# A two-layer decoder trunk in fp32: inputs laid out feature-major, 32-column sample products, and a new order of the first head and of the gate

## The chip, the cores and the metric

The kernel runs on one core of a Trainium2 chip. The metric is the device time of one execution in microseconds. TensorE, VectorE, ScalarE and GpSimd run their own instruction streams and meet at semaphores; SyncE (SP) issues the DMAs. In the profile PE is a TensorE matmul instruction, PEld its weight load, DVE is VectorE, ACT is ScalarE, SPq the queue on SyncE.

## The reference

The trunk has two layers and 1024 features. It takes 528 prompt positions (16 learned meta tokens and 512 tokens) and 8 single sample tokens, each with states of its own. Everything is fp32.

```python
def retention_chunk(q, k, v, s_prev, log_gamma):      # layer 0, 4 heads, dk 256, dv 512
    scores = einsum('bhnd,bhmd->bhnm', q, k) * decay_mask
    inner = einsum('bhnm,bhme->bhne', scores, v)
    cross = einsum('bhnd,bhde->bhne', q, s_prev) * cross_decay
    s_new = exp(log_gamma * L) * s_prev + einsum('bhmd,bhme->bhde', k * k_decay, v)
    return inner + cross, s_new

def retention_mixer(h, ...):
    q, k, v, g = split(h @ w_in)                      # q, k rotated in pairs of features
    o = normalise(retention(q, k, v))                 # mean and variance over dv
    return (silu(g) * o) @ w_out

def shortconv_mixer(h, ...):                          # layer 1
    bg, cg, xin = split(h @ w_in, 3)
    return (bg * dwconv(concat(conv_state, cg * xin))) @ w_out

def conv_ffn(h, ...):                                 # in both layers, d_ff 2816
    up, gate = split(h @ w_in, 2)
    return (silu(dwconv(concat(ffn_state, up)) + b) * gate) @ w_down

for i in range(2):
    x = x + mixer_i(rms_norm(x)); x = x + conv_ffn(rms_norm(x))
return rms_norm(x), new_ret_states, new_conv_rows, new_ffn_rows
```

For a sample the state matters: `cross` is q (1 x 256) times its own 256 x 512 state in each head, and the new state is the decayed old one plus the outer product of k and v. There are 8 x 4 such states of 512 KB each, read and written once.

## The kernel before

The residual `x_res` (X) lies feature-major: 8 tiles of 128 features by 536 columns (528 prompt, 8 sample). A projection is computed as weights (stationary, 128 x 128) times activations (moving, two halves of 260 to 268 columns, `spans`). To keep fp32 accuracy each operand is split into a rounded high part and the rest (`h_hi`, `h_lo`, `w_hi`, `w_lo`), and `three` issues three products of fp32r for each pair of tiles, all accumulating in PSUM: high by high, low by high, high by low. That makes six instructions for one weight tile and one output slot (two banks).

Weights come in units of 128 x 1024 (512 KB). SP loads a unit into one of two slots of `w_raw`, ScalarE rounds it into `w_hi` (L850, `split_hi`), VectorE subtracts into `w_lo` (L1091, `split_lo`), and TensorE uses it from one of four slots. The unit is freed by `unit_done`, and `hi_ready`/`lo_ready` count up to the next load (L273, L277). The order of units, and of every instruction of each engine, is written out by hand; each engine has one program with waits on counts.

The first head. The weights lie in their own row-major arrays, so a unit is gathered by strided DMAs, and the q and k weights are read with a step of two to part the rotary pairs. x arrives as rows in two halves of five DMAs, and small tables (norm gains, conv weights, states) as rows as well. TensorE transposes the tiles of x (L474, 40 instructions) into PSUM, VectorE copies them into X (L1114), ScalarE writes `h_hi` (L855) and the square (L860), VectorE `h_lo` (L1097) and the running sum of squares (L1101, L1104). The queries (`first_q`) are computed between those transposes; `rows_tiles` transposes the tables (L485, L490). `first_k` computes the keys and, between them, the mean of squares (`statistic`, L454) and its row-wise copy (L527). The root, its reciprocal (L1163) and the scaling of the cos and sin tables by it (L1169, L1170) stand ahead of the rotation of Q and K (`rotate`, L1178 to L1181), so q and k are scaled by the norm inside the rotation.

A head. Then come: V (L565, 120 products of 512 columns), the transposes of K (L572), the scores (L587, L595), the KV product for the prompt's state (L602, plain fp32), the inner products of scores and V in four groups `dt` (L633, L635), and the gate: four parts per weight unit and half, units 8 and 9 in one slot pair, 10 and 11 in the other. Q, K, V, scores, states and statistics use plain fp32 or fp32r as the code says. The output projection (units 12 to 15) works on `ret_z_hi` and `ret_z_lo`.

The samples. The eight states of a head pass through a ring of four slots, `state_ring` (S). For each state ScalarE rounds it (`state_hi`, L896) and VectorE takes the rest (`state_lo`, L1210) into `state_split_a` or `_b`; `sample(b)` multiplies it by `dec_q_spread` (QM), in which each sample's q stands in one of 128 columns, as high part in columns 0 to 63 and as low part in 64 to 127. This is

```python
def sample(b):
    pe.wait_ge(s_lo, 8 * h + (b + 1))
    for e in range(2):
        for part in range(2):
            out = mm(PS[:, 1, :], QM[:, e, b * NB:b * NB + P], (SA, SB)[b % 2][:, part, e * DV:(e + 1) * DV], ...)
```

with four fp32r instructions of 512 columns for each sample (L611): two samples ahead of the inner products, one behind each `dt`, two among the gate's first parts. VectorE then updates the state in place (L1249) with the outer product that ScalarE made from v broadcast over the partitions (`outer`, L925); SP stores it (L335) and loads state b + 4 into its slot (L343). ScalarE copies the sums out (`OS`, L942), and a product with `row_sum` (SEL, L658) adds the two rows of each sample and transposes them.

The gate's statistics. TensorE computes the mean over the channels (`statistic(3, MEAN_V, TMP[:, 4, ...])`, L454) after the first pair of parts of unit 9. VectorE subtracts it (L1258), ScalarE squares (L946), VectorE sums (L1263). The second statistic stands between unit 10 and unit 11. Then VectorE: split of unit 12, the gate's scaling (L1267), split of unit 13, the reciprocal of the root (L1288), normalising and the product with silu (L1271, L1277), `z_rest` into `ret_z_lo` (L1281), for which the output projection waits.

The end. After the last FFN TensorE transposes y and the last rows of the FFN's up projection (`state_rows`, L708), and SP stores four blocks of y, y_sample and three DMAs of FFN rows (`ffn_states`).

## Time and profile before

| | before |
|---|---|
| median of 3 runs | 1552.12 us (1551.85 to 1553.26) |
| the profiled execution | 1551.32 us, its span 1549.5 us |
| granted clock of TensorE, mean | 0.998 |
| instructions on TensorE | 11511 matmuls, 11511 weight loads |
| busy share TensorE, VectorE, ScalarE | 99%, 52%, 35% |
| moved by DMA | 171.92 MB, mean 111 GB/s |

The span runs from the first to the last instruction; some microseconds of an execution lie around it. Matmuls overlap, so the time of one is read from the distance of starts, not from its duration. A busy share near 100% says that the engine always had an instruction in hand.

### The profile page before, as it was taken

The numbers are of one execution on the slowest core, as the hardware profiler recorded it, in microseconds if no ns is written. First come the engines' busy times: TensorE is split into PE (matmuls) and PEld (weight loads), VectorE is DVE, ScalarE is ACT, GpSimd is POOL, SyncE is SP. The second block draws the span as 40 slices with busy tenths as digits, with TensorE's granted clock in tenths as the row PEclk, the third lists the DMA queues.
The fourth block names the chain that finished last, engine by engine and source line by source line (L and its number), as shares of the span: only waits on it lengthen the run. The fifth ranks groups of instructions, "written<-read, shape, count | busy, mean of one in ns | idle before, by whom it ended". The sixth has DMA issues, their size and how long they took to land.

```text
span 1549.5 us, 27952 instructions
## 1 busy us (share of the span) xinstructions
PE 1528.8 (99%) x11511; PEld 1458.6 (94%) x11511; DVE 808.7 (52%) x1046; ACT 547.6 (35%) x743; POOL 1.8 (0%) x17
## 2 busy tenths in 40 slices
PE   8999999999999999999999999999999999999997
PEld 7879969987997899999999999999999999999997
DVE  6667437545744696555555233544455555554222
ACT  4264136215412654333333123322333333333222
POOL 0000000000000000000000000000000000000000
PEclk9999999999999999999999999999999999999999
DMA  7362434335252532232232222322322322322321
GB/s 223 101 232 79 161 137 177 124 103 208 81 182 82 218 96 92 85 95 85 91 95 83 94 96 82 96 92 86 96 93 85 95 82 94 95 87 94 96 88 59
DMA packets 119544, 171.92 MB, mean 111 GB/s; under 512 B 5358, under 2 KB 91894, under 8 KB 118382
## 3 DMA queue, kind: packets, MB, share of 16 engines
q1 hardware_dynamic: 119462, 170.71, 33.8%
q8 instruction: 66, 1.08, 0.3%
q14 instruction: 16, 0.13, 0.0%
HBM read 149.35 MB, written 21.55 MB: 110 GB/s over the span
## 4 chain that ended last, share of the span: by engine, by line
PE 97%; DVE 1%; issue 0%; ACT 0%; DMA 0%; SPq 0%; DVEq 0%; ACTq 0%
PE ps L420 79%; PE ps L565 7%; PE ps L633 3%; PE ps L602 2%; PE ps L611 2%; PE ps L595 1%; PE ps L454 1%; PE ps L587 1%; PE ps L474 1%; DMA x_rows<-in_x_sample_dram 0%; PE ps L817 0%; DVE rms L1163 0%; DVE w_lo L1091 0%; PE ps L635 0%; PE ps L658 0%
## 5 line engine op out<-in xcount | busy, mean ns | idle before, releaser
L850 ACT ACTIVATE w_hi<-w_raw 128x1024 fp32r<-128x1024 f32 x228 | 241.1, 1059 | 755.7 <-PE ps L420 663.9
L1091 DVE TENSOR_TENSOR w_lo<-w_raw,w_hi 128x1024 fp32r<-128x1024 f32 x228 | 278.2, 1222 | 387.0 <-ACT w_hi L850 386.9
L420 PE MATMUL ps<-h_hi,w_hi 128*128 128x264 f32 (+2 forms) x2304 | 472.6, 286 | 3.5 <-DVE w_lo L1091 2.8
L420 PE MATMUL ps<-h_lo,w_hi 128*128 128x264 f32 (+2 forms) x2304 | 468.5, 285 | 0.0
L420 PE MATMUL ps<-h_hi,w_lo 128*128 128x264 f32 (+2 forms) x2304 | 468.0, 284 | 0.0
L420 PEld LDWEIGHTS ps<-h_hi,w_hi 128*128 128x128 f32 x2304 | 359.5, 190 | 5.8 <-DVE w_lo L1091 3.0
L420 PEld LDWEIGHTS ps<-h_hi,w_lo 128*128 128x128 f32 x2304 | 358.5, 190 | 0.2 <-issue 0.2
L420 PEld LDWEIGHTS ps<-h_lo,w_hi 128*128 128x128 f32 x2304 | 358.3, 190 | 0.0
L420 PE MATMUL ps<-z_hi,w_lo 128*128 128x264 f32 (+1 forms) x832 | 167.9, 283 | 0.0
L420 PE MATMUL ps<-z_lo,w_hi 128*128 128x264 f32 (+1 forms) x832 | 167.8, 283 | 0.0
L420 PE MATMUL ps<-z_hi,w_hi 128*128 128x264 f32 (+1 forms) x832 | 167.5, 283 | 0.0
L420 PEld LDWEIGHTS ps<-z_hi,w_hi 128*128 128x128 f32 x832 | 128.4, 188 | 0.0
L420 PEld LDWEIGHTS ps<-z_hi,w_lo 128*128 128x128 f32 x832 | 128.2, 188 | 0.0
L420 PEld LDWEIGHTS ps<-z_lo,w_hi 128*128 128x128 f32 x832 | 128.1, 188 | 0.0
L1361 DVE TENSOR_TENSOR tmp<-ps,rms 128x528 f32<-128x528 f32 (+1 forms) x44 | 29.0, 700 | 77.4 <-PE ps L420 77.4
L1342 DVE TENSOR_TENSOR tmp<-ps,rms 128x528 f32<-128x528 f32 (+1 forms) x44 | 29.0, 701 | 69.5 <-PE ps L420 69.5
L565 PE MATMUL ps<-w_hi,h_hi 128*128 128x512 f32 x160 | 63.2, 395 | 0.9 <-DVE tmp L1178 0.9
L565 PE MATMUL ps<-w_hi,h_lo 128*128 128x512 f32 x160 | 63.2, 395 | 0.0
L565 PE MATMUL ps<-w_lo,h_hi 128*128 128x512 f32 x160 | 63.1, 394 | 0.0
L1249 DVE SCALAR_TENSOR_TENSOR state_ring<-state_ring,decay,gate 128x1024 f32<-128x1024 f32 x32 | 40.8, 1283 | 22.7 <-ACT gate L925 20.0
L420 PE MATMUL ps<-ret_z_hi,w_lo 128*128 128x264 f32 x256 | 52.0, 285 | 0.0
L420 PE MATMUL ps<-ret_z_hi,w_hi 128*128 128x264 f32 x256 | 52.0, 284 | 0.0
(177 smaller groups left out, 1379.5 us busy)
## 6 DMA issues: line engine op xcount, KB each, us to landing
w_raw<-in_w_ffn_in_dram SPq DMA_DIRECT2D x88, 512.0 KB, 3.5
w_raw<-in_w_ret_in_dram SPq DMA_DIRECT2D x48, 512.0 KB, 3.7
w_raw<-in_w_ffn_out_dram SPq DMA_DIRECT2D x44, 512.0 KB, 3.7
state_ring<-in_state_ret_dram SPq DMA_DIRECT2D x32, 512.0 KB, 5.5
out_ret_s_dram<-state_ring SPq DMA_DIRECT2D x32, 512.0 KB, 2.9
w_raw<-in_w_sc_in_dram SPq DMA_DIRECT2D x24, 512.0 KB, 3.5
w_raw<-in_w_ret_out_dram SPq DMA_DIRECT2D x16, 512.0 KB, 3.4
v_bcast<-v_scratch SPq DMA_DIRECT2D x8, 1024.0 KB, 5.6
```

The source lines that it names most:

```text
L420: out = mm(PS[:, 2 * s + half, at:at + n_col], a, b[:, lo:lo + n_col], start=first and n == 0, stop=last and n == 2)
L454: out = mm(PS[:, 2 * s + half, at:at + n_col], ones[:], src[:, lo:lo + n_col], start=True, stop=True)
L474: out = pe.transpose(PS[:, 2 * X_SLOT[k] + b // 4, (b % 4) * P:(b % 4) * P + n], XN[0:n, b, k * P:(k + 1) * P], IDENT[0:n, 0:n])
L565: out = mm(PS[:, banks[b], :], a, c, start=k == 0 and q == 0, stop=k == KD - 1 and q == 2)
L602: out = mm(PS[:, 6 + e, :], KN[0:mn, j, e * P:(e + 1) * P], V[0:mn, j, :], start=j == 0, stop=j == 4)
L611: out = mm(PS[:, 1, :], QM[:, e, b * NB:b * NB + P], (SA, SB)[b % 2][:, part, e * DV:(e + 1) * DV], start=b == 0 and e == 0 and part == 0, ...
L633: mm(PS[:, 2 * s + half, a - n0:n1 - n0], V[0:mn, j, vt], PR[0:mn, PCOL[j] + a - m0:PCOL[j] + n1 - m0], start=j == 0, stop=j == js[-1])
L850: fn(WH[:, c % NS, :], RAW[:, c % NR, :], ACT.Copy).then_inc(hi_ready, 1)
L1091: tt(WL[:, c % NS, :], RAW[:, c % NR, :], WH[:, c % NS, :].bitcast(F32), ALU.subtract).then_inc(lo_ready, 1)
L1249: stt(S[:, b % 4, :], S[:, b % 4, :], DEC[:, TP + 5:TP + 6], G[:, at:at + 1024], ALU.mult, ALU.add).then_inc(s_upd, 1)
L1342: tt(halves(TMP[:, t, 0:n_in]), slot(PAIR_A[t], w), halves(R[:, c0:]), ALU.mult).then_inc(up_read, 1)
L1361: tt(halves(TMP[:, t, 0:n_in]), slot(PAIR_B[t], w), halves(R[:, c0:]), ALU.mult).then_inc(gate_read, 1)
```

## The change

Inputs are laid out ahead of the launch: `x_all` (feature-major x), `model_consts` and `ffn_consts` (feature-major tables), and `w_units`, in which each weight unit is one contiguous 128 x 1024 block in the order of its use, with the q and k features parted, so the step of two is gone. x is loaded tile by tile straight into X; unit 0 comes in two halves. The FFN's and the conv's last rows leave in the layout they have on chip and are reordered outside. In the first head the order of units is q and k of the first half, then of the second; keys follow queries with a lag of two tiles; q and k are rotated with unscaled tables and scaled afterwards; the statistic comes after all keys. The samples are computed in two calls of four, unsplit, in plain fp32 with 32 weight columns, each to its own group of 32 partitions. In the gate, three parts of the second slot go first, the second call of samples follows the sixth part, the `SEL` products and the first statistic come later in unit 9. `spans` (264 + 260 columns for 524) is as before.

```diff
+TILE = 32
-X_SETUP = KD
+X_SETUP = 0
+K_LAG = 2
...
-            QM = sb("dec_q_spread", [P, 2, 192], F32R, scope=s2)
+            QM = sb("dec_q_spread", [P, 2, 96], scope=s2)
...
@@ sync: start
-            x_half(0)
-            in_heads(0, 0)
-            x_half(1)
+            sp.dma_start(RAW[:, 0, 0:512], w_all[0, :, 0:512]).then_inc(half_in, 16)
+            x_tile(0)
+            sp.dma_start(CD[:], io["model_consts"]).then_inc(const_in, 16)
+            sp.dma_start(RAW[:, 0, 512:], w_all[0, :, 512:]).then_inc(raw_in[0], 16)
+            x_tile(1)
             in_heads(0, 1)
...
+            x_tile(2)
+            x_tile(3)
+            in_heads(0, 2)
+            x_tile(4)
+            in_heads(0, 3)
+            for k in range(5, KD):
+                x_tile(k)
...
@@ sync: states of a head
-                for b in range(NB):
+                def store(b):
                     sp.wait_ge(s_upd, 8 * h + (b + 1))
...
-                    if b == 4:
-                        sp.wait_ge(kv_ready, h + 1)
...
+                for b in range(4):
+                    store(b)
+                    if b > 0:
+                        reload(b - 1)
+                reload(3)
+                sp.wait_ge(kv_ready, h + 1)
...
+                for b in range(4, NB):
+                    store(b)
...
@@ tensor: first head
+                for k in range(KD):
...
+                    pe.wait_ge(h_lo, k + 1)
+                    for e in range(2):
+                        out = part(2 * (k // 4), PAIR_A[e], k, e)
...
+                    if k >= K_LAG:
+                        n = k - K_LAG
...
+                        part(2 * (n // 4) + 1, PAIR_B[0], n, 0)
...
+                pe.wait_ge(ss_sum, 7)
+                pe.wait_ge(rope, 4)
+                statistic(1, MEAN_D, TMP[:, 2, :], T // 2).then_inc(stat_done, 1)
...
-                    for b in range(5):
+                    for b in ((2, 3, 4, 0, 1) if first else range(5)):
...
+                        if first and n == 4 and b == 0:
+                            pe.wait_ge(rstd, 1)
...
@@ tensor: samples and gate
-                def sample(b):
+                def samples(b0):
...
-                    pe.wait_ge(s_lo, 8 * h + (b + 1))
+                    for c in range(4):
+                        pe.wait_ge(s_in[c], 32 * h + 4 * b0 + 16)
                     for e in range(2):
...
+                        for c in range(4):
+                            at = (b0 + c) * NB
+                            out = mm(PS[TILE * c:TILE * c + TILE, 1, :], QM[:, e, at:at + TILE], S[:, c, e * DV:(e + 1) * DV],
+                                     start=b0 == 0 and e == 0, stop=b0 == 4 and e == 1)
+                    out.then_inc(samp_done, 4)
...
+                samples(0)
...
-                pe.wait_ge(o_ready, 4 * h + 4)
...
+                for n, (kk, e) in enumerate(((0, 1), (1, 1), (2, 1), (0, 0), (1, 0), (2, 0), (3, 0), (3, 1))):
+                    if n == 0:
+                        pe.wait_ge(o_ready, 4 * h + 2)
+                    if n == 3:
+                        pe.wait_ge(o_ready, 4 * h + 4)
+                    out = gate_part(8, PAIR_A, kk, e)
+                    if n == 5:
+                        samples(4)
...
+                    if kk == 0:
+                        pe.wait_ge(sel_ready, 2)
+                        pe.wait_ge(os_ready, h + 1)
...
+                    if kk == 2:
+                        pe.wait_ge(o_sum, 6 * h + 6)
+                        statistic(3, MEAN_V, TMP[:, 4, 0:N_RET], N_RET // 2).then_inc(gstat_done, 1)
...
@@ vector: first head, and updates of the states
+            def first_scale():
...
+                for t in (Q, K):
+                    for e in range(2):
+                        tt(t[:, e, :], t[:, e, :], R[:], ALU.mult).then_inc(qk_scaled, 1)
...
-                    dve.wait_ge(s_lo, 8 * h + (b + 1))
+                    dve.wait_ge(samp_done, 8 * h + 4 * (b // 4 + 1))
...
+                for b in range(4):
+                    update(b)
+                dve.wait_ge(o_ready, 4 * h + 4)
+                channel_sum(slice(C_RET, TP), 0)
+                update(4)
+                update(5)
                 dve.wait_ge(ot_done, h + 1)
...
+                update(6)
+                update(7)
```

On ScalarE `state_hi` goes, `outer(4)` and `outer(5)` follow the first two output copies, and `outer(6)` and `outer(7)` the copy of `OS`. The stores of the FFN's and conv's last rows move from the end into the stream of weight loads, one DMA each.

## Rows read from the trace of the kernel before

**Rows 1.** The page: busy time of TensorE, and the chain by engine.
```profile
PE 1528.8 (99%) x11511; PEld 1458.6 (94%) x11511; DVE 808.7 (52%) x1046; ACT 547.6 (35%) x743; POOL 1.8 (0%) x17
...
PE 97%; DVE 1%; issue 0%; ACT 0%; DMA 0%; SPq 0%; DVEq 0%; ACTq 0%
```

**Rows 2.** Timeline of TensorE, first head: start, duration, line, names, count.
```profile
13.13 0.78 PE L420 MATMUL ps<-h_hi,w_hi 128*128 128x268 f32 x2 [0.69 <-issue]
13.71 0.65 PE L420 MATMUL ps<-h_lo,w_hi 128*128 128x268 f32 x2
...
15.50 0.65 PE L420 MATMUL ps<-h_hi,w_lo 128*128 128x268 f32 x2
...
35.81 1.07 PE L454 MATMUL ps<-tmp,mean_d 128*128 128x268 f32 x4
...
37.73 0.53 PE L420 MATMUL ps<-h_hi,w_hi 128*128 128x268 f32 x2
```

**Rows 3.** The same timeline, V products of the first head and what follows.
```profile
53.69 0.50 PE L565 MATMUL ps<-w_hi,h_hi 128*128 128x512 f32 x1 [0.31 <-DVE tmp L1178]
...
76.10 1.25 PE L572 MATMUL ps<-ident,k_rot 128*128 128x128 f32 x10
```

**Rows 4.** Windows: engines' busy time (instructions), PEclk, DMA share, GB/s.
```profile
0.00:4.00 4.00, 0.98 (x8) 0.93 (x8) 0.34 (x2) 1.49 (x2) 1.83 (x17) 1.00 0.35 80
4.00:8.00 4.00, 0.73 (x4) 0.71 (x4) 0.00 (x0) 0.00 (x0) 0.00 (x0) 1.00 0.98 344
```

**Rows 5.** Timeline of ScalarE and VectorE in the first head.
```profile
9.47 0.74 ACT L855 ACTIVATE h_hi<-x_res,model_consts 128x536 fp32r<-128x536 f32 x1 [7.23 <-DVE x_res L1114]
...
11.80 1.23 DVE L1091 TENSOR_TENSOR w_lo<-w_raw,w_hi 128x1024 fp32r<-128x1024 f32 x1 [0.48 <-ACT w_hi L850]
...
13.57 0.77 DVE L1097 SCALAR_TENSOR_TENSOR h_lo<-x_res,model_consts,h_hi 128x536 fp32r<-128x536 f32 x1
```

**Rows 6.** Timeline of TensorE, second head: first and last of 96 pairs.
```profile
161.70 0.41 PE L420 MATMUL ps<-h_hi,w_hi 128*128 128x268 f32 x2
...
185.36 0.41 PE L420 MATMUL ps<-h_hi,w_lo 128*128 128x268 f32 x2
```

**Rows 7.** Timeline of TensorE, first head: KV product, two samples, what follows.
```profile
82.60 9.43 PE L602 MATMUL ps<-v_rows,k_rows 128*128 128x512 f32 x20
91.96 1.20 PE L611 MATMUL ps<-state_split_a,dec_q_spread 128*128 128x512 f32 x4
...
93.93 2.96 PE L633 MATMUL ps<-scores,v_rows 128*128 128x268 f32 x16
```

**Rows 8.** Timeline of TensorE, second head: both statistics and the output projection.
```profile
257.84 1.06 PE L454 MATMUL ps<-tmp,mean_v 128*128 128x264 f32 x4
...
266.00 1.05 PE L454 MATMUL ps<-tmp,mean_v 128*128 128x264 f32 x4
266.69 0.60 PE L420 MATMUL ps<-h_hi,w_hi 128*128 128x264 f32 x2
...
275.66 0.40 PE L420 MATMUL ps<-ret_z_hi,w_hi 128*128 128x264 f32 x2
```

**Rows 9.** Timeline of VectorE in the same stretch.
```profile
262.20 1.52 DVE L1263 TENSOR_TENSOR tmp<-tmp 128x528 f32<-128x528 f32 x2
...
267.82 3.45 DVE L1288 RECIPROCAL tmp<-tmp 128x528 f32<-128x528 f32 x1 [0.60 <-ACT tmp L863]
...
274.18 0.70 DVE L1281 TENSOR_TENSOR ret_z_lo<-ret_out,ret_z_hi 128x528 fp32r<-128x528 f32 x1
```

**Rows 10.** The page's DMA issues: engine, count, KB each, us to landing.
```profile
state_ring<-in_state_ret_dram SPq DMA_DIRECT2D x32, 512.0 KB, 5.5
out_ret_s_dram<-state_ring SPq DMA_DIRECT2D x32, 512.0 KB, 2.9
```

**Rows 11.** Timeline of the queue on SyncE at the end.
```profile
1543.88 0.72 SPq L402 DMA_DIRECT2D out_y_sample_dram<-y_rows  x1
...
1546.38 0.82 SPq L383 DMA_DIRECT2D out_ffn_s_dram<-ffn_state_rows  x1
```

More of the change, by code:

```diff
@@ L443, in pair_of_k @@
                         for e in range(2):
-                            out = three(slots[e], w, lhs_pair(c + half, kk, e, step),
+                            out = three(slots[e], w, lhs_pair(c + half, kk, e),
                                         h_cols(HH, k, c0, 2 * w), h_cols(HL, k, c0, 2 * w), k == 0, k == KD - 1)
@@ new lines, in head @@
+                for kk in range(4):
+                    for e in range(2):
+                        out = gate_part(9, PAIR_A, kk, e)
+                    if kk == 0:
+                        pe.wait_ge(sel_ready, 2)
+                        pe.wait_ge(os_ready, h + 1)
+                        pe.sem_inc(rows_seen, 1)
+                        for dt in range(4):
+                            row = mm(PS[:, 0, dt * NB:(dt + 1) * NB], OS[:, dt * P:(dt + 1) * P], SEL[:],
+                                     start=True, stop=True)
+                        row.then_inc(ot_done, 1)
+                    if kk == 2:
+                        pe.wait_ge(o_sum, 6 * h + 6)
+                        statistic(3, MEAN_V, TMP[:, 4, 0:N_RET], N_RET // 2).then_inc(gstat_done, 1)
@@ L1506, in shape_constants, with weight_units, put @@
     return {"cos": np.cos(ang).astype(np.float32), "sin": np.sin(ang).astype(np.float32), "decay": decay}
[L1509 to L1511 removed]
+def weight_units(w_ret_in, w_ret_out, w_sc_in, w_sc_out, w_ffn_in, w_ffn_out):
+    units = np.empty((U_ALL, P, UNIT), np.float32)
+    def put(u, block):
+        rows, cols = block.shape
+        units[u] = block.reshape(rows // P, P, cols).transpose(1, 0, 2).reshape(P, UNIT)
+    pairs_apart = np.concatenate([np.arange(0, DK, 2), np.arange(1, DK, 2)])
+    for h in range(HEADS):
+        u = U_HEAD * h
+        for n in range(4):
+            half, part = (n // 2, n % 2) if h == 0 else (n % 2, n // 2)
+            put(u + n, w_ret_in[0, 512 * half:512 * half + 512][:, part * D + h * DK + pairs_apart])
+        for n in range(4):
+            put(u + 4 + n, w_ret_in[0, 256 * n:256 * n + 256, 2 * D + h * DV:2 * D + (h + 1) * DV])
+            at = 2 * D + VDIM + h * DV + 256 * (n // 2)
+            put(u + 8 + n, w_ret_in[0, 512 * (n % 2):512 * (n % 2) + 512, at:at + 256])
+            put(u + 12 + n, w_ret_out[0, h * DV:(h + 1) * DV, 256 * n:256 * n + 256])
+    for l in range(2):
+        for i in range(JF // 2):
+            for n in range(4):
+                at = 256 * i + (n // 2) * DFF
+                put(U_FFN_IN[l] + 4 * i + n, w_ffn_in[l, 512 * (n % 2):512 * (n % 2) + 512, at:at + 256])
+        for n in range(22):
+            g, v = divmod(n, 11)
+            put(U_FFN_OUT[l] + n, w_ffn_out[l, 256 * v:256 * v + 256, 512 * g:512 * g + 512])
+    for i in range(4):
+        for n in range(6):
+            at = 256 * i + (D, 2 * D, 0)[n // 2]
+            put(U_SC_IN + 6 * i + n, w_sc_in[0, 512 * (n % 2):512 * (n % 2) + 512, at:at + 256])
+    for n in range(8):
+        put(U_SC_OUT + n, w_sc_out[0, 512 * (n % 2):512 * (n % 2) + 512, 256 * (n // 2):256 * (n // 2) + 256])
+    return units
```

513 lines of the change are left out of this document (197 added, 316 removed).

## The prediction

> **What bounds the kernel now.** I read the page's busy shares and its chain first. TensorE is busy for 1528.8 us of 1549.5, and the chain that ended last lies on it for 97% [rows 1]. So an edit on VectorE, ScalarE or a queue is worth something only where TensorE waits for it, and a TensorE instruction taken away or added counts in full. The weights' layout in memory, the splits of the states and the fewer VectorE operations are therefore worth nothing by themselves. What is left is four places: the start, where TensorE does its first projection product only at 13.1 us [rows 2]; the sample products inside each of the four heads [rows 7]; the order of the gate with its two statistics [rows 8]; and the tail after the last product [rows 11]. I went through each on the timeline of TensorE, then of the engine that feeds it there.
>
> **Part 1, the start.** Before, x arrives as rows and is transposed 40 times on TensorE; the first product starts at 13.1 us, and the V products end at 76.1 [rows 2, 3]. After, x arrives feature-major, and what the first product needs is half of unit 0 (0.26 MB), tile 0 of x (0.27 MB) and the constants (0.10 MB). The windows show 80 GB/s in the first 4 us, which is 0.32 MB, and 344 GB/s in the next 4 [rows 4]: 0.63 MB is there at 4 + 0.31/0.344 = 4.9 us. Then ScalarE rounds tile 0 (0.74 us) and VectorE takes the rest (0.77 us) [rows 5]: TensorE starts at about 6.5 us, 6.6 us earlier.
>
> From there the work is 8 tiles of x, 4 output slots and 6 instructions each, 192 instructions. Pairs of them follow each other at 0.249 us in a later head (23.66 us for the 95 pairs between its first and its last row), so 0.1245 each, 23.9 us [rows 6]. The first ones go slower: from 13.71 to 15.50 there are four pairs, 0.448 us a pair, 0.224 each [rows 2]. That is what the lower of the two clock levels (1.2 GHz against 2.4) would give, though the window's granted clock reads 1.00 at such a coarse view. Before, this lasted from 13.1 to about 16.8 us; I take the same 3.7 us, in which half the work is lost at 0.1 us for each of 17 instructions, 1.7 us. The queries and keys end at 6.5 + 23.9 + 1.7 = 32.1 us. The statistic and the five row statistics cost 37.73 - 35.81 = 1.9 us, as before [rows 2]: 34.0. V is 120 products; 96 of them ran from 53.69 to 76.10, 0.2334 each [rows 3], 28.0 us: V ends at 62.0 us against 76.1. That is **-14.1 us**.
>
> Can the feeders keep up? For each tile ScalarE rounds and squares, about 0.74 us each, VectorE takes the rest and adds a square, about 0.77 each, and for four units each of them splits, up to 1.23: at most 8 x 1.54 + 4.9 = 17.2 us on VectorE and less on ScalarE [rows 5]. TensorE needs 2.2 us a tile and 25.6 us in all, so it is the slowest after the first tile. All of x and units 0 to 3, 4.3 MB, is in by 4 + 4.0/0.344 = 15.6 us, where tile 7 is wanted at about 22 us [rows 4]. The loads of units 2 and 3 stand in the queue ahead of tiles 4 to 7 and wait for the splits of units 0 and 1, at 6 to 9 us; late by 2 us, they would still be hidden. Before the V products, the late scaling by the root costs VectorE a reciprocal (3.5 us) and six products of 0.7, after the rotation of K at 36 us; that ends at 44 us, and the first that wants it is the transposes of K at 62. So it is hidden; were it not, it would cost 7.7 us once. The bounds: -16 if the first bytes arrive as early as the constants are ready (2.4 us earlier than I took), -11 if each unit's load delays a tile.
>
> **Part 2, the sample products.** Before, one sample is four 512-column instructions; two samples cost 93.93 - 91.96 = 1.97 us [rows 7], so eight cost 7.9 us per head. After, the state isn't split, and the product is plain fp32, with 32 weight columns going to partition groups 0, 32, 64, 96: 16 products per head. Plain fp32 goes in two instructions each: the KV product shows 20 instructions for 10 products, 9.36 us, 0.468 each [rows 7]. So there are 32 instructions of 0.468. No row of before shows products in four column groups, so I bound it.
> - All serial: 32 x 0.468 = 15.0 us per head.
> - All four groups side by side: two calls, two halves e, two passes, 8 x 0.468 = 3.7 us.
> - Pairwise: if instructions start in order and the second pass of a product has to wait for the first one in its own group, the next group's first pass runs beside the second pass of the one before. Eight products take 9 pass times, 4.2 us, both calls 8.4 us.
>
> To each I add 0.2 us for every call, by which the first pair behind a block of plain fp32 is longer (0.60 us at 266.69, where a pair in a row lasts 0.41) [rows 6, 8]. I take the pairwise one, since the passes of a product are adjacent in the stream of [rows 7]: 8.8 against 7.9 us, +0.9 us per head, **+3.7 us**. The ends are -3.8 and +7.5 us per head, -15 and +30 us in all.
>
> The Trainium skill ("TensorE: Matmul & The Clock Gate", the part on packing small matmuls) says that products in different 32-column strips run concurrently, each starting some 4 ns after the one before, and that they start and end strictly in order. No row here shows it; for one instruction per strip it would give the side-by-side case, and for two the pairwise case. Another page ("TensorEngine Tiling (Array Packing)", Key Properties) says that changing the tiling mode drains the engine, which speaks against the edit; it has no price there, and I stay with the 0.2 us.
>
> **Part 3, the order in the gate.** Before, the first statistic comes after the first pair of unit 9's parts, at 257.84, the second one at 266.00, and the output projection at 275.66 [rows 8]. After, the first statistic stands two pairs of parts later (2 x 1.46 = 2.9 us), while all behind it stays. So TensorE has 2.9 us less of other work between the statistic and what comes from it: 5.25 us to the second statistic, and 17.82 - 2.9 = 14.9 us to the projection. VectorE's chain between them: it ends the sum of squares at 263.72, 5.9 us after 257.84, and has the first z_lo ready at 274.88, 17.0 us after. It idled 0.60 us before the reciprocal, for a root that comes earlier now [rows 9], so 16.4 us. TensorE's cover ends before that: 5.9 - 5.25 = 0.65 us at the second statistic and 0.85 more at z_lo, 1.5 us per head, **+6.0 us**. The bounds are 0 (if the four squares or the split behind them go ahead of where they stood) and 2.4 us per head (if the 0.60 isn't given back and z_lo of the third tile is late as well). I take the worked-out value.
>
> The rest of the gate rewrite costs nothing by the rows: three parts now go ahead of the wait for the last output copy. The second call of the samples needs states 4 to 7 back in the ring 16.8 us after the first call ends (four inner groups of 3.1 us and six parts of 0.73). The four updates take 5.2 us, a store 2.9, its successors 3, and a load 5.5 to land [rows 10]: 13.4 to 15.4 us. That is hidden with 1.4 us to spare.
>
> **Part 4, the tail and the middle.** Before, SP issues y_sample at 1543.88 and then three more stores, the last at 1546.38, which leaves 3.1 us to the end at 1549.5 [rows 11]. VectorE's last y rows don't move. After, y_sample is the last store: **-2.5 us**, bounds -1.5 and -3. The transposes of the FFN's last rows go too, a few tenths of a microsecond: costed at nothing.
>
> **Sum.** -14.1 + 3.7 + 6.0 - 2.5 = -6.9 us. The profiled execution took 1551.3 us (span 1549.5), which gives 1544.4; the median of the runs lies 0.8 us above it, so **1545 us**.
>
> **The rivals.**
> - *Four strips side by side.* The samples cost 4.1 us per head, 1545 - 3.7 - 15 = 1526 us. For it: it is what tiles are for. Against: each product is two instructions on the same strip.
> - *Strips don't overlap.* 32 x 0.468 + 0.4 = 15.4 us per head, +30 us where I took +3.7: 1571 us, slower. The samples eat up the other gains from (14.1 - 6.0 + 2.5) / 4 = 2.65 us above the 7.9 of before on, that is from 10.5 us per head. For it: only such rows as [rows 7] exist, all serial. Against: a 32-column product uses a quarter of the array.
> - *The reorder costs nothing*, because VectorE's queue has slack that I took for full: 1539 us.
> - *The second call of the samples waits for the ring.* If the loads land 4 us later than in [rows 10], TensorE stands still 2.6 us per head, and more where the second half of the broadcast is late: 1555 to 1557 us. It decides from 1.4 us of lateness. For it: the loads come in a row behind the stores, and a landing of 5.5 us is a median. Against: one store and the KV copy now come after the last reload.
> - *The start is not gained*, since the queue of loads feeds the eight tiles too slowly: at worst -6.6 us is all that is left, 1552 us, no change.
>
> **How the numbers follow.** Pairwise strips with the gate's wait 0.42; the same without the wait 0.13; side by side 0.16; serial 0.17; the ring late 0.07; the start not gained 0.05. The range from 1526 to 1557 us holds all but the serial case and some edges. Within 0.2% is about 3 us, which is what a measurement of this kernel can tell from no change. Faster: nearly all of the first, the second and the third, 0.71; the same 0.07; slower 0.22.
>
> **What the profile after should show.** The first L420-like product at 6 to 7 us, the last of V at about 62. Per head 32 sample instructions of 32 columns over 8 to 9 us, overlapping in pairs. Idle of TensorE of 0.6 us before the second mean statistic and 0.9 before the products of ret_z. The last store issued near 1537. I am wrong first if the sample products take 4 or 15 us per head, next if the start isn't near 6.5 us.

## The result, and the profile after

| | before | after |
|---|---|---|
| median | 1552.09 us (1551.85 to 1553.26) | 1532.38 us (1531.99 to 1532.77, 4 runs) |
| ratio | | 0.9872, 95% interval 0.9854 to 0.9889 |
| span of the profiled execution | 1549.5 us | 1530.4 us |
| granted clock of TensorE, mean | 0.998 | 0.997 |

The change takes 19.7 us off. The forecast was 1545 us, a gain of 7 us: 12.6 us above the measured time, which lies in the lower part of the stated range (1526 to 1557 us). First the page of the kernel after: busy time, the chain by engine, and the two DMA rows of the ring.

```profile
PE 1504.1 (98%) x11428; PEld 1428.8 (93%) x11428; DVE 765.0 (50%) x1004; ACT 515.7 (34%) x710; POOL 1.7 (0%) x17
...
PE 89%; DMA 4%; DVE 4%; ACT 1%; issue 1%; SPq 0%; DVEq 0%; ACTq 0%
...
state_ring<-in_state_ret_dram SPq DMA_DIRECT2D x32, 512.0 KB, 5.6
out_ret_s_dram<-state_ring SPq DMA_DIRECT2D x32, 512.0 KB, 2.7
```

TensorE was 97% of the chain [rows 1] and is 89% now: DMA and VectorE have come onto it, with 4% each. That says before any timeline that the change didn't only shorten TensorE's work but also opened waits. The idle times of TensorE name them: who waits on which line, for what, us in total, times, the longest.

```profile
PE ps L376 <- DVE h_lo L1024: 7.6, 3, 6.6
PE ps L537 <- DMA state_ring<-in_state_ret_dram: 3.8, 4, 1.6
PE ps L409 <- DVE tmp L1182: 2.4, 4, 0.6
PE ps L376 <- DVE x_res L1231: 2.1, 1, 2.1
PE ps L376 <- DVE ret_z_lo L1200: 2.0, 4, 0.6
```

In the kernel after, L376 is the line of the projections' products (without V), L537 that of the sample products, L409 that of the statistics. The first row is the start. The third and the fifth are the two waits in the gate that were forecast. The second, the samples' second call waiting for the ring in every head, was a rival only. The fourth happens once, at the end of the second head, and before had a like one (its stretch there took 26.33 us against 23.36 in the others, and takes 25.87 against 23.59 now).

Right behind it TensorE's granted clock falls to 0.50, the lower of its two levels (1.2 GHz of 2.4), for 3.4 us (in the line of this window it is the third number from the end):

```profile
287.00:290.40 3.40, 3.40 (x16) 3.40 (x16) 0.19 (x1) 0.00 (x0) 0.00 (x0) 0.50 0.55 182
```

The stretch from there to V takes 25.32 us where it takes 23.69 in the other heads, 1.6 us more. The kernel before has the same dip (25.65 against 23.90), so it plays hardly any part in the 19.1 us; but some of the executions below lack it, and are shorter by as much.

Now the timeline of TensorE, start to the end of the first head, to be laid beside [rows 2, 3, 7, 8].

```profile
6.58 0.79 PE L376 MATMUL ps<-h_hi,w_hi 128*128 128x268 f32 x2 [6.58 <-DVE h_lo L1024]
...
9.76 0.81 PE L376 MATMUL ps<-h_hi,w_hi 128*128 128x268 f32 x2 [0.15 <-DVE h_lo L1024]
...
12.65 0.48 PE L376 MATMUL ps<-h_hi,w_hi 128*128 128x268 f32 x2 [0.82 <-DVE h_lo L1024]
...
33.75 1.06 PE L409 MATMUL ps<-tmp,mean_d 128*128 128x268 f32 x4
...
35.67 0.50 PE L487 MATMUL ps<-w_hi,h_hi 128*128 128x512 f32 x1
...
64.00 1.25 PE L496 MATMUL ps<-ident,k_rot 128*128 128x128 f32 x10
...
79.87 1.93 PE L537 MATMUL ps<-state_ring,dec_q_spread 128*32 128x512 f32 x16
81.72 3.06 PE L558 MATMUL ps<-scores,v_rows 128*128 128x268 f32 x16
...
98.77 0.40 PE L376 MATMUL ps<-h_hi,w_lo 128*128 128x264 f32 x2
99.74 1.92 PE L537 MATMUL ps<-state_ring,dec_q_spread 128*32 128x512 f32 x16 [0.57 <-DMA state_ring<-in_state_ret_dram]
101.60 0.51 PE L376 MATMUL ps<-h_hi,w_hi 128*128 128x264 f32 x2
...
114.44 1.13 PE L409 MATMUL ps<-tmp,mean_v 128*128 128x264 f32 x4 [0.60 <-DVE tmp L1182]
...
124.91 0.48 PE L376 MATMUL ps<-ret_z_hi,w_hi 128*128 128x264 f32 x2 [0.60 <-DVE ret_z_lo L1200]
```

What the reader is to see: the V products end at 64.0 us where they ended at 76.1; a call of sixteen sample instructions takes 81.72 - 79.87 = 1.85 us; and three gaps open behind it, which each cost some 0.2 us more than their bracket (the idle time) says, since pairs follow each other at 0.245 us (98.77 to 99.74 is 0.97, so 0.73 are lost). Of such a figure at a sample call some 0.08 us are there without any wait: so much is left wherever the states are in time.

Where the 19.1 us of span went, from the starts of the same steps in both timelines:

| stretch | before | after | difference |
|---|---|---|---|
| to the end of V, first head | 76.10 | 64.00 | -12.1 |
| transposes of K to the gate, 4 heads | 34.38, 34.32, 34.31, 34.38 | 30.55, 30.48, 30.49, 30.55 | -15.3 |
| gate to the output projection, 4 heads | 27.86 x3, 27.87 | 30.36, 30.38, 30.59, 31.36 | +11.2 |
| the rest of the heads | | | -0.5 |
| layer 1 and the FFNs, to the transposes of y | 955.83 | 955.50 | -0.3 |
| from there to the end | 15.2 | 13.1 | -2.1 |
| sum | | | -19.1 |

### The profile page after: what moved, and what is told of

Same layout as the page of the kernel before. It is cut to its first block, busy times and chain, and to the rows that moved or that the text cites. A ratio compares the mean times of both kernels' runs of the same rounds, so it can differ in the third digit from the quotient of the medians.

```text
span 1530.4 us, 27659 instructions
## 1 busy us (share of the span) xinstructions
PE 1504.1 (98%) x11428; PEld 1428.8 (93%) x11428; DVE 765.0 (50%) x1004; ACT 515.7 (34%) x710; POOL 1.7 (0%) x17
## 4 chain that ended last, share of the span: by engine, by line
PE 89%; DMA 4%; DVE 4%; ACT 1%; issue 1%; SPq 0%; DVEq 0%; ACTq 0%
PE ps L376 76%; PE ps L487 7%; PE ps L526 2%; DMA out_ret_s_dram<-state_ring 2%; DMA state_ring<-in_state_ret_dram 1%; PE ps L537 1%; DVE tmp L1207 1%; PE ps L519 1%; DVE w_lo L999 1%; PE ps L511 1%; ACT tmp L860 1%; PE ps L409 0%; DMA w_raw<-in_w_units_dram 0%; DVE ret_out L1190 0%; DVE ret_out L1177 0%
## 5 line engine op out<-in xcount | busy, mean ns | idle before, releaser
L376 PE MATMUL ps<-h_hi,w_hi 128*128 128x264 f32 (+2 forms) x2304 | 473.0, 287 | 9.7 <-DVE h_lo L1024 7.6
L376 PE MATMUL ps<-h_lo,w_hi 128*128 128x264 f32 (+2 forms) x2304 | 468.6, 285 | 0.0
L376 PE MATMUL ps<-h_hi,w_lo 128*128 128x264 f32 (+2 forms) x2304 | 467.3, 284 | 0.0
L376 PEld LDWEIGHTS ps<-h_hi,w_hi 128*128 128x128 f32 x2304 | 357.7, 189 | 14.6 <-issue 12.2
L376 PEld LDWEIGHTS ps<-h_lo,w_hi 128*128 128x128 f32 x2304 | 357.7, 189 | 0.0
L376 PEld LDWEIGHTS ps<-h_hi,w_lo 128*128 128x128 f32 x2304 | 357.6, 189 | 0.0
L376 PE MATMUL ps<-z_hi,w_lo 128*128 128x264 f32 (+1 forms) x832 | 167.9, 283 | 0.0
L376 PE MATMUL ps<-z_lo,w_hi 128*128 128x264 f32 (+1 forms) x832 | 167.8, 283 | 0.0
L376 PE MATMUL ps<-z_hi,w_hi 128*128 128x264 f32 (+1 forms) x832 | 167.5, 283 | 0.0
L376 PEld LDWEIGHTS ps<-z_hi,w_hi 128*128 128x128 f32 x832 | 128.4, 188 | 0.0
L376 PEld LDWEIGHTS ps<-z_hi,w_lo 128*128 128x128 f32 x832 | 128.2, 188 | 0.0
L376 PEld LDWEIGHTS ps<-z_lo,w_hi 128*128 128x128 f32 x832 | 128.0, 188 | 0.0
L840 ACT ACTIVATE gate<-v_bcast,dec_k 128x512 f32<-128x512 f32 x64 | 41.4, 713 | 45.5 <-DMA v_bcast<-v_scratch 33.5
L376 PE MATMUL ps<-ret_z_hi,w_hi 128*128 128x264 f32 x256 | 52.6, 287 | 2.0 <-DVE ret_z_lo L1200 2.0
```

Of the source, the lines that this page charges most:

```text
L376: out = mm(PS[:, 2 * s + half, at:at + n_col], a, b[:, lo:lo + n_col], start=first and n == 0, stop=last and n == 2)
L840: fn(G[:, at:at + DV], VB[:, b, :], ACT.Copy, scale=KD8[:, e, b:b + 1]).then_inc(samp_kv, 1)
```

## The experiments

**How far do the strips run side by side?** A strip is one of the four groups of 32 partitions to which a product of 32 weight columns writes. Three kernels differ from the one after in the order or the place of the sample products. In the first, all products of a call go to the partitions 0 to 31; in the second, to two strips. Both sum samples together that belong apart, so their sample outputs are not the reference's; the sample products and their operands are the same, and the copy and the `SEL` products behind them take only the partitions that were written.

```diff
# one_strip
-out = mm(PS[TILE * c:TILE * c + TILE, 1, :], QM[:, e, at:at + TILE], ...
-         start=b0 == 0 and e == 0, stop=b0 == 4 and e == 1)
+out = mm(PS[0:TILE, 1, :], QM[:, e, at:at + TILE], ...
+         start=b0 == 0 and e == 0 and c == 0, stop=b0 == 4 and e == 1 and c == 3)
# two_strips
+out = mm(PS[TILE * (c % 2):TILE * (c % 2) + TILE, 1, :], QM[:, e, at:at + TILE], ...
+         start=b0 == 0 and e == 0 and c < 2, stop=b0 == 4 and e == 1 and c > 1)
# strip_by_strip
-                    for e in range(2):
-                        for c in range(4):
+                    for c in range(4):
+                        for e in range(2):
```

> The changed kernel, but all four products of a sample call go to the same 32 partitions (the sums of the four samples are mixed, so this output is not the reference's; the rest is as it was). Theory A, column strips work side by side: a call of 16 instructions took 1.9 us because four strips ran at once; on one strip they follow each other at 0.468 us, 7.5 us a call, 5.6 us more, twice in four heads: +45 us, about 1577 us. Theory B, a plain-fp32 instruction with 32 weight columns is short by itself (0.12 us), wherever it goes: no change, 1532 us.

> The same, but the four products alternate between two groups of 32 partitions (sums of two samples each are mixed, so this output is not the reference's). Theory A: 16 instructions over two strips, 8 pass times of 0.468 = 3.7 us a call, 1.9 us more than with four: +15 us, about 1547 us. Theory B: 1532 us.

> The changed kernel with the two loops of a sample call exchanged: four instructions in a row for strip 0, then four for strip 1, and so on. Same products, same strips. Theory C (that of my prediction, starts in order, and a pass waits for the one before it on its strip): only the last pass of a strip overlaps the first of the next, 13 pass times, 6.1 us a call, 4.2 us more: +34 us, about 1566 us. Theory D, the strips take their work independently of the order in the stream: no change, 1532 us.

One run each: 1572.98 us, 1545.74 us and 1530.64 us. The timeline of TensorE at the first call, for one strip,

```profile
80.13 7.05 PE L537 MATMUL ps<-state_ring,dec_q_spread 128*32 128x512 f32 x16
87.11 3.06 PE L558 MATMUL ps<-scores,v_rows 128*128 128x268 f32 x16
```

for two strips (its call lasts to 83.25),

```profile
79.69 3.63 PE L537 MATMUL ps<-state_ring,dec_q_spread 128*32 128x512 f32 x16
```

and for four, ordered strip by strip:

```profile
80.17 1.94 PE L537 MATMUL ps<-state_ring,dec_q_spread 128*32 128x512 f32 x16
82.05 3.06 PE L558 MATMUL ps<-scores,v_rows 128*128 128x268 f32 x16
```

So a call takes 6.98, 3.56 and 1.88 us, and 1.85 in the kernel after: about halved with each doubling of the strips. On one strip an instruction costs 6.98 / 16 = 0.44 us (the expectation had taken 0.468), on four 0.12. The 1530.64 us of the third kernel are no gain by its order: its profiled span is 1.7 us shorter than that of the kernel after, and in it the clock didn't fall behind the second head (23.80 us from there to V instead of 25.32). The last kernel decides between the forecast's mechanism and its rival. With two halves of two passes each on one strip, adjacent in the stream, instructions that start in order would leave little to overlap; yet the call is as short as before. The trace, asked for the sample instructions that touch 80.22 to 80.60 us (in flight; count, duration ns, first and last start), shows four already at work together in this kernel too:

```profile
L537 PE MATMUL ps<-state_ring,dec_q_spread x4: 617/617/617, 80.2 to 80.2; 128*32 128x512 f32 x4
```

The next four start at 80.6, then at 81.1 and 81.5. On one strip alone the trace has one start every 0.43 us, so four that start together are on four strips. The records don't name the strip, but they do show that the order of the stream had changed: within a four the starts lie 13 to 14 ns apart here and 7 ns in the kernel after, twice as far with twice as many instructions of one strip in a row. The pairwise case, on which the forecast rests, falls: a second pass does wait for the first one on its own strip, but it doesn't hold up what stands behind it for another strip. That each strip works off its own instructions is my reading of this; that the order of the two loops makes no difference to the time of a call is measured. The Trainium skill ("TensorE: Matmul & The Clock Gate", the part on packing small matmuls) says that products in different strips run concurrently; the runs agree, and with two passes a product as well. The Trainium skill says in the same part that products start strictly in order, each some 4 ns after the one before. Four starts together, out of a stream with four instructions in a row for each strip, do not bear out the order, and the distances are 7 and 13 to 14 ns.

**The samples and the gate without the rest.** The kernel before, with the sample calls, ring order, state updates and gate of the one after; inputs, first head and tail stay.

```diff
 # samples_and_gate_only, against the kernel before
-C_LO = 64
+TILE = 32
-QM = sb("dec_q_spread", [P, 2, 192], F32R, scope=s2)
+QM = sb("dec_q_spread", [P, 2, 96], scope=s2)
# and in short: sample(b) on SA, SB, state_hi and state_lo go;
# samples(0), samples(4) on S come; store, reload, update, outer and the gate's order as after
```

> The kernel before with only the new samples (unsplit, 32 columns, two calls, ring order, updates) and the new gate order; inputs, weight loads, first head's start and the end are those of before. If the changed kernel's trace is read rightly, the heads gave 4.6 us and the start and end the other 14 to 15: the profiled span falls from 1549.5 by 4 to 6 us, the ratio is 0.996 to 0.997. Rival: the gains of samples show only with contiguous loads, because the strided loads crowd the ring's reloads: then the ring wait before the second call grows and the time is that of before or above it.

1547.96 us in the median of 8 runs (1545.86 to 1549.61) against 1552.07, ratio 0.9974 (0.9963 to 0.9985), a little above the 0.996 to 0.997 expected; the profiled span fell by 5.0 us, as expected. It is a gain by itself, where the forecast booked 9.7 us of loss for these two parts. In its trace the first V products end 2.6 us later than before, with the transposes of x starting only at 9.16 us behind a load of x's rows; the transposes of K to the gate take 30.54, 30.49, 30.49 and 30.55 us, as after, and the gate 30.04, 29.60, 31.33 and 29.72. These two stretches gain 6.1 us here and 4.1 in the kernel after, whose ring waited longer (4.4 us against 2.3). So the gain of the heads is this part's, and the start's 12 us, which are not there, belong to the other part.

**The kernel after once more**, beside three kernels that each move one thing in the gate, timed on the same chip.

```diff
 # second_call_later
-                    if n == 5:
+                    if n == 7:
                         samples(4)
 # stat_earlier
-                    if kk == 2:
+                    if kk == 1:
                         statistic(3, MEAN_V, TMP[:, 4, 0:N_RET], N_RET // 2)
 # unit13_later (VectorE)
-                split_lo(NS + 9, U_HEAD, h)
                 dve.wait_ge(g_std, h + 1)
...
                 z_rest(1)
+                split_lo(NS + 9, U_HEAD, h)
                 normalise(2)
```

> The changed kernel once more, beside the three that follow, so that they are compared on one chip: 1532 us, ratio 0.987.

> The changed kernel with the second sample call behind all eight parts of unit 8 and not behind six: 1.46 us more cover for the ring. In the changed kernel TensorE waits 0.7, 0.7, 1.1 and 1.9 us there. Theory A, what follows hangs on VectorE's chain that starts with this call (updates, mean, z_lo), so that a later call moves all of it: the ring wait goes, the waits at the second statistic and at z_lo grow by as much, and only the head with 1.9 us gains: 0 to 1 us less, 1531 to 1532 us. Theory B, each wait counts by itself: 4 us less, 1528 us.

> The changed kernel with the first statistic of the gate one pair of parts (1.46 us) earlier. VectorE now idles 0.69 us for it after the last update. Theory A (chain): that idle time is what can be gained, so the two waits of TensorE (0.76 and 0.77 us per head) fall to some 0.8 in sum: 2.8 us less, 1529.5 us. Theory B, the waits are the missing cover of 1.46 us in full: both vanish, 6 us less, 1526 us. Theory C, no gain, since the root or the squares on ScalarE set the end.

> The changed kernel, in which VectorE splits unit 13 behind the second z_lo and not ahead of the reciprocal: the split is 1.14 us of VectorE's chain before the first z_lo, and unit 13 is wanted 2.9 us after the projection starts. Theory A (chain): the wait at the projection (0.77 us per head) goes, that at the second statistic stays: 3 us less, 1529 us. Theory B: the wait only moves to the products of unit 13 or to the third z_lo: no change, 1532 us.

| kernel | median (runs), us | ratio to before | gate to projection, 4 heads |
|---|---|---|---|
| changed_again | 1531.32 (1530.51 to 1531.84) | 0.9871 (0.9855 to 0.9888) | 30.80, 29.58, 29.83, 30.07 |
| second_call_later | 1528.79 (1528.35 to 1528.97) | 0.9853 (0.9837 to 0.9870) | 29.80, 29.65, 29.64, 30.00 |
| stat_earlier | 1528.67 (1527.88 to 1530.45) | 0.9857 (0.9841 to 0.9874) | 29.81, 28.83, 29.36, 29.54 |
| unit13_later | 1531.59 (1531.19 to 1532.04) | 0.9871 (0.9855 to 0.9888) | 29.68, 29.89, 29.48, 29.96 |

The ring's wait differs from execution to execution: by the distances of the starts TensorE lost 0.73, 0.87, 1.07 and 1.73 us there in the first profile of the kernel after, and 1.18, 0.09, 0.28 and 0.43 in that of `changed_again`. So gains of one or two microseconds are read from the waits as well as from the medians.

*The second call two parts later* gives 2.5 us, between the 0 to 1 us of the one theory and the 4 us of the other. The waits of TensorE in it:

```profile
PE ps L409 <- DVE tmp L1182: 2.4, 4, 0.6
PE ps L376 <- DVE ret_z_lo L1200: 2.0, 4, 0.6
```

Both are as they were, and the ring's wait is down to 0.2 us, from 1.3 in the same view of `changed_again`; by the distances of the starts it is 0.6 after 2.0. Of the 1.6 us between the two profiled spans 1.3 are thus the ring's. That the rest of the 2.5 us between the medians is the ring's too is likely, since its wait varies so much, and not shown. A wait for the ring is not paid back at the statistic: what arrives late there stays lost.

*The statistic one pair of parts earlier* gives 2.7 us, as its theory A had it: the wait at the second statistic (2.4 us) is gone, the one at `ret_z_lo` is not. The term of the forecast for the first of the two waits is shown.

*The split of unit 13 out of the way* removes the wait at `ret_z_lo` (2.6 us by the distances) and gains nothing. Its waits:

```profile
PE ps L376 <- DVE gate L1186: 2.8, 4, 0.7
PE ps L537 <- DMA state_ring<-in_state_ret_dram: 2.7, 4, 0.9
```

TensorE now stands still inside the projection, for the fourth part of the gate, which VectorE scales 1.2 us later behind the moved split; from the projection to the next head it takes 24.3 us instead of 23.6, 2.5 us over the four heads. VectorE is full there (in the first head of the kernel after it has no gap above 0.1 us from 111.5 to 129 us), and a wait taken away at one product comes back at the next.

**The first call of the samples ahead of the KV product**, so that the ring has 9.4 us more. On ScalarE the KV copy goes behind the four outer products, or it would wait for a product that is now later.

```diff
 # first_call_earlier (TensorE)
                 pe.wait_ge(kn_ready, 5 * h + 5)
+                pe.wait_ge(qm_ready, 3 * h + 3)
+                samples(0)
...
                 out.then_inc(kv_done, 1)
-                pe.wait_ge(qm_ready, 3 * h + 3)
-                samples(0)
 # (ScalarE)
-                act.wait_ge(kv_done, h + 1)
-                fn(KV[:], PS[:, 6:8, :], ACT.Copy).then_inc(kv_ready, 1)
                 outer(2)
                 outer(3)
+                act.wait_ge(kv_done, h + 1)
+                fn(KV[:], PS[:, 6:8, :], ACT.Copy).then_inc(kv_ready, 1)
```

> The changed kernel with the first sample call ahead of the KV product, and ScalarE's copy of the KV sums behind the fourth outer product, so that the updates can start as soon as v is broadcast and not 3.2 us later: the ring's stores and reloads go 3 us earlier. Theory A, the second call waits for the chain of updates, stores and reloads: its waits of 0.7 to 1.9 us go, 4.4 us less (1527.5 us). Theory B, the reloads wait for the DMA engines, which are full in that stretch whatever the order: at most 1 us less.

> The changed kernel with the three: first call ahead of the KV product, first statistic one pair earlier, unit 13 split later. If each gives what its theory A says and none stands in another's way: 4.4 + 2.8 + 3.1 = 10.3 us less, about 1522 us, ratio to before 0.980 to 0.981. If they share a chain, less than the sum: 1525 us.

1526.34 us (1525.95 to 1527.51, 5 runs), ratio 0.9842 (0.9828 to 0.9855), with no wait for the ring left in its trace: 5.0 us below changed_again, 4.5 by the ratios. Not all of that is the ring's. Of the 4.3 us between the two profiled spans (1528.5 and 1524.2), the gates hold 1.6 (30.07 to 29.68 in the mean), the stretches from the transposes of K to the gate 0.5, the start 0.5, and 1.5 lie in the stretch from the second head's end to the next V (25.31 against 23.80), where the edit touches nothing. Those 1.5 us are the clock: in this execution it stayed up, though TensorE had stood still for 2.35 us just before, longer than the 2.11 us ahead of the dip in the kernel after.

```profile
287.00:290.40 3.40, 3.40 (x29) 3.40 (x29) 0.00 (x0) 0.00 (x0) 0.00 (x0) 1.00 0.84 280
```

In `first_and_stat`, below, the clock falls to 0.50 again from 284.8 to 288.2 us, and the stretch takes 25.30. The five executions of `first_call_earlier` fall into two groups accordingly: spans of 1524.1 and 1524.2 us at a mean granted clock of 0.999, and of 1525.4 and 1525.5 at 0.998. What the early call is worth lies between the 1.6 us of the gates and the 4.4 that the ring took in the first profile of the kernel after.

`all_three` (this, `stat_earlier` and `unit13_later` together) ran in 1523.47 us (1523.39 to 1525.65), ratio 0.9823 (0.9810 to 0.9836): some 8 us gained of the 10.3 that the sum of the parts gave. In its trace the gate takes 28.2 us in each head, and the wait for `gate` is there again with 2.7 us in 4.

**Without the moved split.** The last two kernels leave the split of unit 13 where it was: `first_and_stat` is `first_call_earlier` with `kk == 1`, and `first_stat_second` has `n == 7` besides.

> The kernel after, with the first call of the samples ahead of the KV product (the KV copy behind the four outer products on ScalarE) and the first mean statistic one pair of parts earlier; the split of unit 13 stays ahead of the gate's scaling, other than in all_three. Theory A, the two waits that go are independent and the split of unit 13 moved away buys nothing: first_call_earlier (1526.3) minus the 2.4 to 2.7 us of the wait at the second statistic, so 1524 us, with the wait for ret_z_lo (2.0 us in 4) still there, no wait for the gate, projection to next head 23.6 us; 1523 to 1524.5 and equal to all_three. Theory B, the split of unit 13 in its old place lengthens VectorE's chain again once the statistic is early: the wait for ret_z_lo grows to 4 us in 4, and 1526 us.

> first_and_stat, and the second call of the samples behind the last of unit 8's parts instead of behind the sixth. The wait for the ring is gone already with the first call in its new place. Theory A, the move of the second call was worth its 2.5 us in second_call_later by the ring's wait alone: now no change, within 0.5 us of first_and_stat. Theory B, it has a gain of its own (fewer changes between products): another 1.5 to 2.5 us, 1521.5 to 1522.5 us.

1524.92 us (1523.87 to 1525.21), ratio 0.9827 (0.9813 to 0.9841), and 1524.36 us (1524.11 to 1525.22), ratio 0.9825 (0.9811 to 0.9839). The traces are as the first theories had them: the wait for `ret_z_lo` stays, that for the ring and that at the statistic are gone. The times are a little beside their bounds (1523 to 1524.5 us, and within 0.5 us of each other). What the early call and the early statistic give adds up, and the second call's place is worth nothing that these runs can tell once the ring is in time. The waits of `first_and_stat`:

```profile
PE ps L376 <- DVE h_lo L1023: 7.2, 1, 7.2
PE ps L376 <- DVE w_lo L998: 2.5, 1, 2.5
PE ps L376 <- DVE ret_z_lo L1199: 2.0, 4, 0.6
```

The intervals of these two and of `all_three` overlap, so none of them is the best; all three stand about 0.5% below the kernel after (0.9825 / 0.9872). In the profiled executions, which all three have the dip of the clock, `all_three` spans 1523.7 us and the other two 1522.5 and 1522.4: the moved split shows no gain there either.

## Why the prediction was right or wrong

| step | forecast | measured |
|---|---|---|
| Part 1, the start | -14.1 | -12.1 |
| Part 2, the sample products | +3.7 | -16.7 |
| Part 3, waits at the statistic and at z_lo | +6.0 | +5.7 |
| Part 3, the ring | 0 | +4.4 |
| gate and inner groups beside these | 0 | +2.5 |
| the heads' rest and the middle | 0 | -0.8 |
| Part 4, the tail | -2.5 | -2.1 |
| sum (of the unrounded terms) | -6.9 | -19.1 |

**Part 2 failed, and it alone decides the size.** "I take the pairwise one, since the passes of a product are adjacent in the stream" was the choice. The two calls of a head take 1.85 and 1.86 us, 3.7 in all where 8.8 were forecast and 7.9 stood before: -4.2 us per head, -16.7. That is the rival of four strips side by side, whose term of -15 the forecast had worked out and given 0.16. The rule behind the choice has two halves, and no row supported either. That a second pass waits for the first one on its strip holds: `one_strip` has one start every 0.43 us. That everything behind it in the stream waits with it fails: in the kernel after and in `strip_by_strip` four start together. The price at a change of shape, taken as 0.2 us a call, is 0.1: the first pair behind a call takes 101.95 - 101.60 = 0.35 us where others take 0.245.

**Part 1 was right in its mechanism and 2.0 us too large.** The first product came at 6.58 us, forecast 6.5, and the statistic and row statistics took 35.67 - 33.75 = 1.92 us, forecast 1.9. The queries and keys ended at 33.75, not 32.1. TensorE waited for `h_lo` twice, and by the distances of the pairs lost 0.37 us at 9.76 and 0.98 at 12.65. The text had weighed the engines' sum of work against TensorE's; it should have gone through their order. ScalarE, in its own timeline, had stood still for the loads of the second half of unit 0 and of unit 1, each with a tile behind it (the rounding of tile 1 at 8.08 us, of tile 2 at 10.90),

```profile
7.31 0.63 ACT L794 ACTIVATE w_hi<-w_raw 128x512 fp32r<-128x512 f32 x1 [1.80 <-DMA w_raw<-in_w_units_dram]
8.08 0.74 ACT L790 ACTIVATE h_hi<-x_res,model_consts 128x536 fp32r<-128x536 f32 x1
9.39 1.06 ACT L763 ACTIVATE w_hi<-w_raw 128x1024 fp32r<-128x1024 f32 x1 [0.57 <-DMA w_raw<-in_w_units_dram]
10.36 0.64 ACT L786 ACTIVATE x_squares<-x_res 128x536 f32<-128x536 f32 x1
10.90 0.73 ACT L790 ACTIVATE h_hi<-x_res,model_consts 128x536 fp32r<-128x536 f32 x1
```

and VectorE has the split of unit 1 ahead of its tile 2:

```profile
10.49 1.23 DVE L999 TENSOR_TENSOR w_lo<-w_raw,w_hi 128x1024 fp32r<-128x1024 f32 x1 [0.78 <-ACT w_hi L763]
11.73 0.78 DVE L1024 SCALAR_TENSOR_TENSOR h_lo<-x_res,model_consts,h_hi 128x536 fp32r<-128x536 f32 x1
```

The tile that TensorE wants at 11.7 us is ready at 12.5. The forecast's bound of -11 had named this, a load of a unit that delays a tile, and its sum had left it out. Another 0.3 us are the V products, 28.3 us against 28.0; the last 0.2 are spread over the rest. This reading of the queue was not tried in a run. The 1.7 us for the slow start held: until 10.4 us the pairs are some 0.45 us apart (7.17, 7.61, 8.06), then 0.25. The windows read a granted clock of 1.00 there, but where they read 0.50, behind the second head, the pairs are just as far apart (287.29, 287.74, 288.18), so the lower level, as the forecast took it, is the likely reading.

**Part 3 was right for the two waits.** By the distances of the starts each head loses 0.76 us at the second statistic, and 0.77, 0.57, 0.59 and 0.71 at z_lo, where 0.65 and 0.85 were forecast: 5.7 us over four heads. The sum is closer than its terms, of which one was too small and one too large. `stat_earlier` took the first of them away and got its 2.7 us. It is the kind of step that the timelines carry well: all instructions were in the trace of before, and only their order changed.

**The ring was costed at nothing and cost 4.4 us** in this execution (2.0 in the other). The rival was there (0.07) with the point from which it decides, 1.4 us of lateness. That slack was wrong in the sum itself: the four terms written down, 5.2 us for the updates, 2.9 for a store, 3 for its successors and 5.5 for a load, add up to 16.6 us and not to 13.4 to 15.4, so only 0.2 of the 16.8 us were left. The rows were the second flaw: a median over 32 transfers [rows 10] stood for the ones that end the chain. The chain of work in head 1 of the kernel after, in order of time (start, duration, what):

```profile
217.86 1.29 DVE state_ring L1159
...
220.37 2.74 DMA out_ret_s_dram<-state_ring
...
223.80 6.34 DMA out_ret_s_dram<-state_ring
...
230.30 5.46 DMA state_ring<-in_state_ret_dram
```

The first call ends at 217.72. Until the store of state 1 is issued, 2.65 us go by, and it takes 2.74. The store of state 3 stands in the queue behind the reload that waits for that store; it took 6.34 us where the median is 2.7, with two reloads and another store issued in the 1.8 us ahead of it. The last reload landed 235.76 - 217.72 = 18.0 us after the first call's end; the cover by TensorE's own rows was 17.3 us. That the other transfers in flight made the store slow is how I read the queue, and no run tried it alone; that the wait goes when the call comes earlier, `first_call_earlier` shows.

**Beside these**, the stretch from the transposes of K to the gate holds 0.2 us a head more than the sample products explain, and the gate 0.4. In the third head the 0.2 us lie in the inner products, whose sixteen instructions take 2.92 us now and 2.81 before, four times a head; the samples that stood between them had cost 0.1 us each more than the one in a row. Why stays open. From the first product of a head to V it takes 23.69 us instead of 23.90, and `samples_and_gate_only`, with the old layout of the weights, keeps the 23.90. So the new inputs gave 0.2 us a head: not the nothing that was forecast, but little. **Part 4** gave 2.1 of its 2.5 us; y_sample is the last issue of the queue on SyncE, 4.1 us ahead of the end.

```profile
1523.02 2.89 SPq L358 DMA_DIRECT2D out_y_prompt_dram<-y_rows  x4
1526.30 0.80 SPq L360 DMA_DIRECT2D out_y_sample_dram<-y_rows  x1
```

## What to carry to other kernels

Where the decisive cost has no row in the trace and its bounds are 4 and 15 us a head, the middle is not safer than an end: a mechanism argued from the order of the stream needs a row of its own, and without one the ends deserve the larger part of the chance. A buffer's return trip is the sum of what each transfer takes at that moment, and here one store in it took 6.3 us where the page's median is 2.7; so add the terms up once more, and take a slack of a tenth of the trip for none. Before two medians are compared to a microsecond, the clock's row in both traces belongs beside them: one dip of 3.4 us is worth 1.5. And before an operation is moved off a full engine's path, ask which result stands behind its new place: the moved split removed one wait of 0.65 us a head and brought another of the same size.

## What the runs showed of the hardware

- Plain fp32 products with 32 weight columns, each in two instructions, run four at a time on four strips: 16 instructions in 1.85 us, 3.56 on two strips, 6.98 on one. The rate of one strip, 0.44 us an instruction of 512 columns, is near the 0.468 of a full-width one [rows 7]: where 32 weight columns are enough, four instructions with different moving data go in the time of one.
- Instructions of different strips needn't alternate in the stream: with four in a row on each strip the call took 1.88 us, and four started within 40 ns.
- TensorE's granted clock fell to 0.50 for 3.4 us behind a standstill of 2.1 us at the end of the second head, in the kernel after (287.0 to 290.4 us) and in nine of the other thirteen profiled executions; in `first_call_earlier` it stayed at 1.00 behind a standstill of 2.35 us. The stretch was 1.5 us longer with it, the pairs 0.45 us apart instead of 0.25.
- A 512 KB store of a state took 2.7 us in the median and 6.34 us in one case, as the fourth of the ring's burst.
